# Output projection: the first chunk's mean subtracted by VectorE out of a bank, in place of a product per chunk

## The chip, the cores and the metric

One core of one Trainium2 chip runs the whole program. The metric is the device time of one execution in microseconds. Five engines work side by side, each on its own queue and ordered against the others by semaphores: TensorE (PE: products; PEld: its weight loads), VectorE (DVE), ScalarE (ACT), GpSimd (POOL) and SyncE (SP, which issues the loads of weights). Products land in banks of PSUM, each of 512 fp32 numbers in each of 128 partitions; VectorE and ScalarE read them there.

## The reference, cut to what matters

The kernel is one layer of an encoder for 512 new frames (with 16 meta tokens ahead of them) and 64 frames of a running stream: a layer norm, the input projection, a pooling branch and stick-breaking attention, gates, the output projection, a second layer norm, an MLP and a third layer norm. The change touches the output projection and the layer norm behind it:

```
mix = sigmoid(ga) * (pool_out @ w_br_pool) + sigmoid(gb) * (attn @ w_br_attn)
h   = _layer_norm(ALPHA * h + (mix @ w_out + b_out), ln1_g, ln1_b)

def _layer_norm(x, g, b):
    mu  = mean(x, axis=-1)
    var = mean(square(x - mu), axis=-1)
    return (x - mu) * rsqrt(var + LN_EPS) * g + b
```

A layer norm does not change when the same number is subtracted from all 1024 channels of a token. The kernel uses that: it takes the mean of the first 128 channels off all of them before it sums their squares.

## The kernel before, in words

Activations are kept transposed: channels on the 128 partitions, in 8 chunks (KC = 8), and the 576 tokens (TA) along the free dimension, in two halves of 288 (HA). For accuracy each fp32 operand is split in two parts, hi and lo, and each product of a 128x128 block of weights is three: hi x hi, hi x lo, lo x hi (`kept`, lines 972 to 974). One chunk of output for one half of the tokens is so 8 x 3 = 24 products with 288 columns each.

`out_pass(h)` (line 983) computes the output projection for token half h: out chunks m = 0 to 7, each into bank m % 2 of `lin`. TensorE starts a chunk when the weights are split (`lo_split`, first pass only) and when its bank is free (`bank_free`), which VectorE reports after it has added chunk m - 2 to the residual (`out_half`, line 2137). With two banks VectorE has about one chunk of time for each.

The residual r1 is ready before the projection: ScalarE and VectorE make ALPHA * h + b_out there. `out_half(m, h)` adds the bank to it. After chunk 0, ScalarE writes the negated chunk 0 of the residual into `first_r` (`first_chunk`, line 1491). `ones_r` holds 1/128 everywhere, so the product of ones_r with first_r is the negated mean of the first 128 channels, on every partition. In the kernel before, TensorE adds this product to the bank of every chunk m = 1 to 7 (line 1000) as the last of its accumulation, and once per half into a bank of its own, `r1_shift(h)` (line 1003), out of which VectorE adds it to chunk 0 (`first_shifted`, line 2146). `r1_shift(0)` is bank 2 of `z`, `r1_shift(1)` is `small`.

From the shifted residuals ScalarE makes squares (`square1`), GpSimd sums them and the residuals (`add1`), and TensorE multiplies the two sums by 1/1024 (`r1_sums`). For the first half that product stands behind chunk 0 of the second pass; for the second half it stands behind the first tile of the MLP. VectorE then takes the variance, centres, makes the inverse root and scales chunk by chunk, and ScalarE and VectorE write h_hi and h_lo for the MLP (`norm1_hi`, `norm1_lo`). For the first half all of this lies on VectorE between the evacuations of the second pass, in an order written out by hand (lines 2246 to 2271), along with the splits of the first MLP weights. In the first pass VectorE's queue holds the splits of the projection's weights (`split_out`) and two parts of the residual (`residual_lo`). Before the first `first_chunk`, ScalarE makes the last two parts of its residual and loads a table of functions (lines 1486 to 1495).

Of the kernel before, what the change touches and what calls it, by code (L numbers as in the profile page):

```python
# [8 lines left out]
ALU = mybir.AluOpType  # L9
# [11 lines left out]
KC = D_MODEL // P  # L21
# [135 lines left out]
def encoder_step(nc, x, wstream, w2_d, vecs_d, bv_d, kc_d, vc_d, state_d, wpool_d, y_out, k_out, v_out, s_out):  # L157
    with ExitStack() as ctx:
        base = 16512

        def sb(name, shape, dt, at):

            return nc.alloc_sbuf_tensor_at(name, [P] + shape, dt, offset=base + 4 * at)

        def sem(name):
            return ctx.enter_context(nc.semaphore(name))
# [41 lines left out]
        mix_hi = sb("mix_hi", [KC, TA], F32R, A0 + 13824)  # L208
        mix_lo = sb("mix_lo", [KC, TA], F32R, A0 + 23360)
# [25 lines left out]
        r1 = sb("r1", [KC, TA], F32, A0)  # L235
# [4 lines left out]
        first_r = sb("first_r", [TA], F32R, A0 + 27968 + 7 * TA)  # L240
        ones_r = sb("ones_r", [P], F32R, A0 + 32576)
# [60 lines left out]
        n0_mean, n0_guess, n0_rstd = sem("n0_mean"), sem("n0_guess"), sem("n0_rstd")  # L302
        n0_centred_v, n0_centred_g, n0_scaled, n0_hi, n0_lo = (
            sem("n0_centred_v"), sem("n0_centred_g"), sem("n0_scaled"), sem("n0_hi"), sem("n0_lo"))
        n1_prep1, n1_prep, n1_first, n1_shift, n1_d0 = (
            sem("n1_prep1"), sem("n1_prep"), sem("n1_first"), sem("n1_shift"), sem("n1_d0"))
        n1_sq, n1_sum, n1_sumsq, n1_terms = sem("n1_sq"), sem("n1_sum"), sem("n1_sumsq"), sem("n1_terms")
        n1_msq, n1_mean, n1_var, n1_guess, n1_rstd = (
            sem("n1_msq"), sem("n1_mean"), sem("n1_var"), sem("n1_guess"), sem("n1_rstd"))
# [69 lines left out]
        def vec(col):  # L379
            return vecs[:, bass.ds(col, 1)]  # L380
# [58 lines left out]
        def out_bank(m, p):  # L439

            if m < KEPT2:
                return p, N_MLP2 + m
            i = (KC - KEPT2) * p + m - KEPT2
            return i % 2, N_MLP2 + KEPT2 + i // 2
# [20 lines left out]
        def half(h):  # L465
            return slice(h * HA, (h + 1) * HA)

        def out_home(m):

            if m < 2:  # L470
                return whi[:, m, :], wlo[:, m, :]
            return stay_hi[m // 2 - 1][:, m % 2, :], stay_lo[m // 2 - 1][:, m % 2, :]

        def mlp1_home(j):

            if j < 2:
                return whi[:, j, :], wlo[:, j, :]
            return stay_hi[1][:, j - 2, :], stay_lo[1][:, j - 2, :]
# [7 lines left out]
        def r1_mean(h):  # L486
            return z[:, h, 0:HA]
# [4 lines left out]
        def r1_shift(h):  # L492
            return z[:, 2, 0:HA] if h == 0 else small[:, 0:HA]
# [102 lines left out]
        def _(pe):  # L596
# [372 lines left out]
            def kept(out, home, k, hi, lo, first, last):  # L969

                w_h, w_l = home[0][:, bass.ts(k, P)], home[1][:, bass.ts(k, P)]
                pe.matmul(out, w_h, hi, start=first, stop=False)  # L972
                pe.matmul(out, w_h, lo, start=False, stop=False)  # L973
                return pe.matmul(out, w_l, hi, start=False, stop=last)  # L974

            def r1_sums(h):

                pe.wait_ge(n1_sum, 7 * (h + 1))
                pe.matmul(r1_mean(h), inv_d[:, :], sum1[:, half(h)], start=True, stop=True)
                pe.wait_ge(n1_sumsq, 7 * (h + 1))  # L980
                pe.matmul(r1_sq(h), inv_d[:, :], sumsq1[:, half(h)], start=True, stop=True).then_inc(n1_terms, 1)

            def out_pass(h):

                c = half(h)
                for m in range(KC):
                    bank = lin[:, m % 2, 0:HA]
                    if h == 0:
                        pe.wait_ge(lo_split, U_OUT + m + 1)
                    pe.wait_ge(bank_free[m % 2], N_OUT + 4 * h + m // 2)  # L990
                    for k in range(KC):
                        if m == 0:
                            pe.wait_ge(mix_lo_done, 2 * k + h + 1)
                        last = kept(bank, out_home(m), k, mix_hi[:, k, c], mix_lo[:, k, c], k == 0,
                                    m == 0 and k == KC - 1)
                    if m:
                        if m == 1:
                            pe.wait_ge(ones_made, 1)
                            pe.wait_ge(n1_first, h + 1)
                        last = pe.matmul(bank, ones_r[:, :], first_r[:, c], start=False, stop=True)  # L1000
                    last.then_inc(unit_done if h else half_done, 1)
                    if m == 1:
                        pe.matmul(r1_shift(h), ones_r[:, :], first_r[:, c], start=True, stop=True)\
                            .then_inc(n1_shift, 1)
                    if h == 1 and m == 0:
                        r1_sums(0)

# [3 lines left out]
            def mlp1_kept(j, h, k):  # L1011

                c = slice(META + h * HA, META + (h + 1) * HA)
                return kept(lin[:, j % 2, 0:HA], mlp1_home(j), k, h_hi[:, k, c], h_lo[:, k, c], k == 0, k == KC - 1)

            for j in range(4):
                pe.wait_ge(lo_split, U_MLP1[0] + j + 1)
                pe.wait_ge(bank_free[j % 2], N_MLP1[0] + j // 2)
                for k in range(KC):
                    if j == 0:  # L1020
                        pe.wait_ge(n1_lo, k + 1)
                    last = mlp1_kept(j, 0, k)
# [3 lines left out]
            for k in range(KC + LAG):  # L1026
                if k < KC:
# [3 lines left out]
                    last = mlp1_kept(0, 1, k)  # L1031
                    if k == KC - 1:
                        last.then_inc(unit_done, 1)
                if k >= LAG:
                    if k == LAG:
                        pe.wait_ge(bank_free[1], N_MLP1[0] + 2)
                    last = mlp1_kept(1, 1, k - LAG)
            last.then_inc(unit_done, 1)
            for j in range(2, 4):
                pe.wait_ge(bank_free[j % 2], N_MLP1[0] + 3)  # L1040
                for k in range(KC):
                    last = mlp1_kept(j, 1, k)
# [82 lines left out]
            for m in range(KEPT2):  # L1125
                for h in range(2):
                    bank, before = out_bank(m, h)
# [8 lines left out]
            for p, c in enumerate(PARTS2):  # L1136
                for m in range(KEPT2, KC):
                    bank, before = out_bank(m, p)
# [626 lines left out]
        def _(dve):  # L1765
            tt = nc.vector.tensor_tensor
# [17 lines left out]
            def split_kept(u, home):  # L1784

                dve.wait_ge(hi_split, u + 1)
                tt(home[1], raw[:, u % RAW, :], home[0].bitcast(F32), ALU.subtract).then_inc(lo_split, 1)
# [174 lines left out]
            for m in range(4):  # L1962
# [4 lines left out]
                for e in range(2):  # L1967
                    rows = slice(64 * e, 64 * e + 64)
                    last = nc.vector.tensor_scalar(q_s[rows, 2 * m + e, :], lin[rows, 1, SEQ - HA:HA],
                                                   vecs[rows, V_BIN + C_Q + m:V_BIN + C_Q + m + 1], SB_SCALE,  # L1970
                                                   ALU.add, ALU.mult)
# [135 lines left out]
            def split_out(m):  # L2107
                split_kept(U_OUT + m, out_home(m))

            def residual_lo(m):  # L2110

                dve.wait_ge(n1_prep1, m + 1)
                stt(out=r1[:, m, :], in0=h_lo[:, m, META:T].bitcast(F32), scalar=ALPHA, in1=r1[:, m, :],
                    op0=ALU.mult, op1=ALU.add).then_inc(n1_prep, 1)
# [22 lines left out]
            def out_half(m, h):  # L2137

                if h == 0:
                    dve.wait_ge(half_done, N_OUT + m + 1)  # L2140
                    dve.wait_ge(n1_prep, m + 1)
                else:
                    dve.wait_ge(unit_done, U_OUT + m + 1)
                tt(r1[:, m, half(h)], lin[:, m % 2, 0:HA], r1[:, m, half(h)], ALU.add).then_inc(bank_free[m % 2], 1)

            def first_shifted(h):

                dve.wait_ge(n1_shift, h + 1)
                tt(r1[:, 0, half(h)], r1_shift(h), r1[:, 0, half(h)], ALU.add).then_inc(n1_d0, 1)
# [10 lines left out]
            def centre1(h):  # L2160


                dve.wait_ge(n1_mean, h + 1)
                for k in range(BY_DVE1):
                    tt(r1[:, k, half(h)], r1[:, k, half(h)], r1_mean(h), ALU.subtract).then_inc(n1_centred_v, 1)
# [21 lines left out]
            def norm1_lo(k, h):  # L2187

                cc = slice(META + h * HA, META + (h + 1) * HA)
                dve.wait_ge(n1_hi, KC * h + k + 1)  # L2190
                stt(out=h_lo[:, k, cc], in0=r1[:, k, half(h)], scalar=vec(V_LN1_B + k),
                    in1=h_hi[:, k, cc].bitcast(F32), op0=ALU.add, op1=ALU.subtract).then_inc(n1_lo, 1)
# [41 lines left out]
            def split_mlp1(j):  # L2234
                split_kept(U_MLP1[0] + j, mlp1_home(j))

            split_out(2)
            for m in range(KC):
                out_half(m, 0)
                if m in (1, 2):  # L2240
                    residual_lo(5 + m)
                if m == 1:
                    first_shifted(0)
                if m + 3 < KC:
                    split_out(m + 3)
            out_half(0, 1)
            split_mlp1(0)
            variance1(0)
            centre1(0)
            out_half(1, 1)  # L2250
            first_shifted(1)
            inverse1(0)
# [1 line left out]
            scale1(1, 0)  # L2254
            norm1_lo(0, 0)
            split_mlp1(1)
            out_half(2, 1)
            for k in (2, 3, 4):
                scale1(k, 0)
                norm1_lo(k - 1, 0)  # L2260
            out_half(3, 1)
            for k in (5, 6, 7):
                scale1(k, 0)
                norm1_lo(k - 1, 0)
            out_half(4, 1)
            norm1_lo(7, 0)
            split_mlp1(2)
            out_half(5, 1)
            split_mlp1(3)
            out_half(6, 1)  # L2270
            out_half(7, 1)

            first_tile(0, 0)
# [449 lines left out]
```

## Time and profile before

| | us |
|---|---|
| median of 3 runs | 816.35 (815.94 to 817.53) |
| profiled execution | 816.22 |
| its span | 814.2 |
| TensorE busy | 799.0 (98%) |
| VectorE busy | 495.2 (61%) |
| ScalarE busy | 388.9 (48%) |
| GpSimd busy | 100.3 (12%) |
| mean granted TensorE clock | 0.995 of full speed |
| first pass of the projection, first product | 354.63 |
| second pass, first product | 381.04 |
| first product of the MLP | 408.60 |

The span is the time from the first to the last instruction of the profile; the execution's own time is about 2 us longer. The last three lines are points of time from the span's start, read in the timeline. Products are pipelined: the profile gives each a duration of 0.29 us, though the next one starts well before it ends. An engine's busy time counts overlapped instructions once. In a timeline a bracket at the end of a row says how long the engine was idle ahead of it and for whom it waited.

### The profile page before, as it was taken

The page shows a single profiled execution, that of the slowest core. Times are in us where ns is not written, and L with a number is a line of the kernel's source. Part 1 is how long each engine was busy: PE and PEld are TensorE (multiplying, and loading weights), DVE is VectorE, ACT ScalarE, POOL GpSimd, SP SyncE. Part 2 cuts the span into 40 slices and gives each one's busy share as a digit, 9 for nine tenths or more (in the row PEclk, how much of TensorE's full clock was granted, in tenths as well). Part 3 has the DMA queues.
Part 4 walks back from the last instruction along what each step waited for, and adds up shares of the span by engine and source line. Part 5 has one row for each costly group of instructions (what it writes and reads, how often), then busy time and mean ns, then how long its engine had stood idle before and what let it go on. Part 6 is the DMA issues. An engine that isn't in the chain of part 4 may idle for free.

```text
span 814.2 us, 14502 instructions
## 1 busy us (share of the span) xinstructions
PE 799.0 (98%) x5892; PEld 767.9 (94%) x5893; DVE 495.2 (61%) x829; ACT 388.9 (48%) x646; POOL 100.3 (12%) x120
## 2 busy tenths in 40 slices
PE   8999999999999999999999999999999999999994
PEld 6999899988988899999999999999999999999994
DVE  5823454553535376874977678775667877445444
ACT  4623345554646475563555663334455333344334
POOL 2100000660000000006720000000000000000444
PEclk9999999999999999999999999999999999999997
DMA  8632131112111112243202214222321422223102
GB/s 297 264 135 84 52 112 52 59 50 78 53 52 53 52 52 78 79 131 104 85 20 78 65 39 155 79 104 78 100 69 39 155 78 105 78 79 95 60 14 103
DMA packets 23081, 71.61 MB, mean 88 GB/s; under 512 B 2464, under 2 KB 6704, under 8 KB 22640
## 3 DMA queue, kind: packets, MB, share of 16 engines
q1 hardware_dynamic: 22336, 68.23, 25.2%
q0 software_dynamic: 544, 2.52, 0.9%
q8 instruction: 40, 0.66, 0.3%
q14 instruction: 17, 0.14, 0.1%
q10 hardware_dynamic: 144, 0.07, 0.0%
HBM read 65.96 MB, written 4.85 MB: 87 GB/s over the span
## 4 chain that ended last, share of the span: by engine, by line
PE 96%; DVE 2%; ACT 1%; DMA 1%; issue 0%; SPq 0%; ACTq 0%; DVEq 0%
PE lin L603 14%; PE lin L604 14%; PE lin L605 14%; PE z L1067 6%; PE z L1069 5%; PE z L1070 5%; PE z L840 3%; PE lin L972 3%; PE lin L973 3%; PE lin L974 3%; PE lin L1088 2%; PE lin L1086 2%; PE lin L1087 2%; PE z L826 1%; PE z L901 1%; PE lin L723 1%
## 5 line engine op out<-in xcount | busy, mean ns | idle before, releaser
L603 PE MATMUL lin<-h_hi,whi 128*128 128x288 f32 (+1 forms) x832 | 247.3, 297 | 0.0
L604 PE MATMUL lin<-h_lo,whi 128*128 128x288 f32 (+1 forms) x832 | 245.9, 296 | 0.0
L605 PE MATMUL lin<-h_hi,wlo 128*128 128x288 f32 (+1 forms) x832 | 245.0, 294 | 0.0
L605 PEld LDWEIGHTS lin<-h_hi,wlo 128*128 128x128 f32 x832 | 156.6, 188 | 0.0
L603 PEld LDWEIGHTS lin<-h_hi,whi 128*128 128x128 f32 x832 | 156.4, 188 | 0.1
L604 PEld LDWEIGHTS lin<-h_lo,whi 128*128 128x128 f32 x832 | 156.4, 188 | 0.1
L1772 DVE TENSOR_TENSOR wlo<-raw,whi 128x1024 fp32r<-128x1024 f32 x65 | 80.9, 1245 | 34.9 <-ACT whi L1162 30.0
L1162 ACT ACTIVATE whi<-raw 128x1024 fp32r<-128x1024 f32 x58 | 60.9, 1051 | 50.5 <-PE lin L605 32.5
L1565 ACT ACTIVATE relu_t<-lin,vecs 128x288 f32<-128x288 f32 x60 | 30.0, 500 | 91.4 <-PE lin L605 88.0
L2196 DVE TENSOR_TENSOR relu_sq<-relu_t 128x288 f32<-128x288 f32 x60 | 27.4, 457 | 64.8 <-ACT relu_t L1565 64.8
L1067 PE MATMUL z<-f_ops,whi 128*128 128x288 f32 x216 | 64.0, 296 | 1.0 <-issue 1.0
L1069 PE MATMUL z<-f_ops,whi 128*128 128x288 f32 x216 | 63.5, 294 | 0.0
L1070 PE MATMUL z<-f_ops,wlo 128*128 128x288 f32 x216 | 63.0, 291 | 0.0
L1612 ACT ACTIVATE whi<-w_set 128x768 fp32r<-128x768 f32 x36 | 30.4, 846 | 52.8 <-PE z L1070 42.5
L2643 POOL TENSOR_TENSOR sum<-r 128x576 f32<-128x576 f32 x1 | 1.4, 1438 | 346.4 <-DVE r L2417 346.4
L1067 PEld LDWEIGHTS z<-f_ops,whi 128*128 128x128 f32 x216 | 40.5, 188 | 1.4 <-issue 1.4
L1070 PEld LDWEIGHTS z<-f_ops,wlo 128*128 128x128 f32 x216 | 40.7, 188 | 0.0
L2335 DVE TENSOR_TENSOR wlo<-w_set,whi 128x768 fp32r<-128x768 f32 x36 | 34.5, 957 | 10.0 <-ACT whi L1612 10.0
L1069 PEld LDWEIGHTS z<-f_ops,whi 128*128 128x128 f32 x216 | 40.5, 188 | 0.0
L1991 DVE SCALAR_TENSOR_TENSOR sa<-z,sa 128x512 f32<-128x512 f32 (+4 forms) x25 | 19.8, 793 | 26.9 <-ACT sa L1338 26.9
L1069 PE MATMUL z<-f_ops,third_hi 128*128 128x288 f32 x120 | 35.6, 297 | 0.0
L1070 PE MATMUL z<-f_ops,third_lo 128*128 128x288 f32 x120 | 35.2, 293 | 0.0
(338 smaller groups left out, 1887.5 us busy)
## 6 DMA issues: line engine op xcount, KB each, us to landing
raw<-w_stream SPq DMA_DIRECT2D x88, 512.0 KB, 3.5
w_set<-w_sets SPq DMA_DIRECT2D x32, 384.0 KB, 3.7
r<-x_t SPq DMA_DIRECT2D x8, 296.0 KB, 5.0
kcache<-k_cache SPq DMA_DIRECT2D x1, 2048.0 KB, 10.2
vcache<-v_cache SPq DMA_DIRECT2D x1, 2048.0 KB, 10.3
y<-r SPq DMA_DIRECT2D x8, 160.0 KB, 1.8
k_new<-k_t POOLq DMA_DIRECT2D x1, 1184.0 KB, 4.8
v_new<-v_t POOLq DMA_DIRECT2D x1, 1024.0 KB, 5.2
```

The lines of the kernel that those rows point to most:

```text
L603: pe.matmul(out, w_h, hi, start=first, stop=False)
L604: pe.matmul(out, w_h, lo, start=False, stop=False)
L605: return pe.matmul(out, w_l, hi, start=False, stop=last)
L1067: pe.matmul(out, w_h, f_op(f, i, 0), start=opens and i == 0, stop=False, skip_group_check=True)
L1069: pe.matmul(out, w_h, f_op(f, i, 1), start=False, stop=False, skip_group_check=True)
L1070: last = pe.matmul(out, w_l, f_op(f, i, 0), start=False, stop=i == PRS - 1, skip_group_check=True)
L1162: nc.scalar.activation(whi[:, j % SPLIT, :], raw[:, j, :], ACT.Copy).then_inc(hi_split, 1)
L1565: nc.scalar.activation(dst, lin[:, bank, 0:HA], ACT.Relu, bias=vec(V_B1 + u)).then_inc(bank_free[bank], 1)
L1612: nc.scalar.activation(op_home(o)[0], w_set[g % 2][:, i, :], ACT.Copy).then_inc(s_hi, 1)
L1772: tt(wlo[:, j % SPLIT, :], raw[:, j, :], whi[:, j % SPLIT, :].bitcast(F32), ALU.subtract)\
L2196: tt(dst, src, src, ALU.mult).then_inc(f_sq_done, 1)
L2335: tt(home[1], w_set[g % 2][:, RAW_SLOT[q], :], home[0].bitcast(F32), ALU.subtract).then_inc(s_lo, 1)
```

## The change

The product per chunk is gone. The one product of ones_r and first_r that is left goes into the bank r1_shift(h), and stands in the middle of chunk 1 (after k = 3) in place of behind it; the wait for first_r moves with it. VectorE adds that bank to the residual of each of the chunks 1 to 7 in an instruction of its own, `shifted1(m, h)`, which waits for the shift product and for the residual to be prepared, and reports to a new semaphore `n1_shifted`. `out_half(m, h)` waits for it. In VectorE's hand-written order the first half's additions of chunks 1 and 2 stand ahead of out_half(1, 0), those of chunks 3 to 7 behind out_half(1, 0) to out_half(5, 0); in the second half shifted1(1, 1) and shifted1(2, 1) stand directly ahead of their out_half, and shifted1(m, 1) for m = 3 to 7 behind out_half(m - 1, 1).

```diff
                     for k in range(KC):
                         if m == 0:
                             pe.wait_ge(mix_lo_done, 2 * k + h + 1)
-                        last = kept(bank, out_home(m), k, mix_hi[:, k, c], mix_lo[:, k, c], k == 0,
-                                    m == 0 and k == KC - 1)
-                    if m:
-                        if m == 1:
+                        if m == 1 and k == KC // 2:
                             pe.wait_ge(ones_made, 1)
                             pe.wait_ge(n1_first, h + 1)
-                        last = pe.matmul(bank, ones_r[:, :], first_r[:, c], start=False, stop=True)
+                            pe.matmul(r1_shift(h), ones_r[:, :], first_r[:, c], start=True, stop=True)\
+                                .then_inc(n1_shift, 1)
+                        last = kept(bank, out_home(m), k, mix_hi[:, k, c], mix_lo[:, k, c], k == 0, k == KC - 1)
                     last.then_inc(unit_done if h else half_done, 1)
-                    if m == 1:
-                        pe.matmul(r1_shift(h), ones_r[:, :], first_r[:, c], start=True, stop=True)\
-                            .then_inc(n1_shift, 1)
...
+                if m:
+                    dve.wait_ge(n1_shifted, 7 * h + m)
                 tt(r1[:, m, half(h)], lin[:, m % 2, 0:HA], r1[:, m, half(h)], ALU.add).then_inc(bank_free[m % 2], 1)
+
+            def shifted1(m, h):
+
+                dve.wait_ge(n1_shift, h + 1)
+                dve.wait_ge(n1_prep, m + 1)
+                tt(r1[:, m, half(h)], r1_shift(h), r1[:, m, half(h)], ALU.add).then_inc(n1_shifted, 1)
...
             for m in range(KC):
+                if m == 1:
+                    shifted1(1, 0)
+                    first_shifted(0)
+                    shifted1(2, 0)
                 out_half(m, 0)
                 if m in (1, 2):
                     residual_lo(5 + m)
-                if m == 1:
-                    first_shifted(0)
+                if m and m + 2 < KC:
+                    shifted1(m + 2, 0)
                 if m + 3 < KC:
                     split_out(m + 3)
...
             centre1(0)
+            shifted1(1, 1)
             out_half(1, 1)
...
             split_mlp1(1)
+            shifted1(2, 1)
             out_half(2, 1)
+            shifted1(3, 1)
...
             out_half(3, 1)
+            shifted1(4, 1)
...
             out_half(4, 1)
+            shifted1(5, 1)
...
             out_half(5, 1)
+            shifted1(6, 1)
             split_mlp1(3)
             out_half(6, 1)
+            shifted1(7, 1)
             out_half(7, 1)
```

## Rows read from the trace of the kernel before

**Rows 1.** Page, part 1: busy us (share of span) xinstructions, by engine
```profile
PE 799.0 (98%) x5892; PEld 767.9 (94%) x5893; DVE 495.2 (61%) x829; ACT 388.9 (48%) x646; POOL 100.3 (12%) x120
```

**Rows 2.** Waits of PE over the whole span: us in total, times, longest
```profile
PE lin L720 <- ACT h_hi L1257: 1.4, 1, 1.4
```

**Rows 3.** Windows: length, busy us (xcount) by engine, PEclk (granted), DMA
```profile
15.00:20.00 5.00, 2.99 (x14) 1.93 (x13) 4.24 (x10) 2.53 (x6) 2.86 (x9) 1.00 0.79 268
381.04:408.60 27.56, 27.56 (x206) 27.35 (x205) 20.49 (x37) 13.47 (x26) 17.30 (x18) 1.00 0.24 76
805.00:810.00 5.00, 0.00 (x0) 0.00 (x0) 4.90 (x14) 3.06 (x8) 2.56 (x4) 0.56 0.07 26
```

**Rows 4.** Line 1000: duration ns min/median/max, first and last start
```profile
L1000 PE MATMUL lin<-first_r,ones_r x14: 292/294/297, 361.0 to 408.5; 128*128 128x288 f32 x14
```

**Rows 5.** Timeline of PE, first pass, chunk 1: start us, us
```profile
357.83 0.29 PE L972 MATMUL lin<-mix_hi,whi 128*128 128x288 f32 x1
359.43 0.29 PE L972 MATMUL lin<-mix_hi,whi 128*128 128x288 f32 x1
361.02 0.29 PE L1000 MATMUL lin<-first_r,ones_r 128*128 128x288 f32 x1
361.28 0.30 PE L972 MATMUL lin<-mix_hi,stay_hi 128*128 128x288 f32 x1
```

**Rows 6.** Timeline of PE, second pass, and first product of the MLP
```profile
384.21 0.65 PE L979 MATMUL z<-sum,inv_d 128*128 128x288 f32 x2
386.75 0.30 PE L972 MATMUL lin<-mix_hi,whi 128*128 128x288 f32 x1
...
395.27 0.29 PE L972 MATMUL lin<-mix_hi,stay_hi 128*128 128x288 f32 x1
401.94 0.29 PE L972 MATMUL lin<-mix_hi,stay_hi 128*128 128x288 f32 x1
408.60 0.29 PE L972 MATMUL lin<-h_hi,whi 128*128 128x288 f32 x1
```

**Rows 7.** Timeline of ACT: before and at the negated copies of chunk 0
```profile
358.92 1.28 ACT L1182 ACT_TABLE_LOAD   x1
360.21 0.45 ACT L1494 ACTIVATE first_r<-r 128x288 fp32r<-128x288 f32 x1
...
385.43 0.43 ACT L1494 ACTIVATE first_r<-r 128x288 fp32r<-128x288 f32 x1
```

**Rows 8.** Timeline of DVE, second pass
```profile
389.36 0.44 DVE L2149 TENSOR_TENSOR r<-small,r 128x288 f32<-128x288 f32 x1
389.73 0.44 DVE L2171 SCALAR_TENSOR_TENSOR sumsq<-var,sumsq 128x288 f32<-128x288 f32 x1
390.21 0.95 DVE L2174 SCALAR_TENSOR_TENSOR z<-sumsq,rstd 128x288 f32<-128x288 f32 x1
...
393.89 0.45 DVE L2144 TENSOR_TENSOR r<-lin,r 128x288 f32<-128x288 f32 x1
...
397.74 1.03 DVE L2191 SCALAR_TENSOR_TENSOR h_lo<-r,vecs,h_hi 128x288 fp32r<-128x288 f32 x1
...
400.53 0.44 DVE L2144 TENSOR_TENSOR r<-lin,r 128x288 f32<-128x288 f32 x1
...
403.27 0.44 DVE L2144 TENSOR_TENSOR r<-lin,r 128x288 f32<-128x288 f32 x1
```

**Rows 9.** Timeline of POOL: last sum of squares of the first half
```profile
382.54 0.80 POOL L2621 TENSOR_TENSOR sumsq<-sumsq,sq 128x288 f32<-128x288 f32 x1
```

**Rows 10.** Timeline of PE and DVE: restarts of PE after waits
```profile
17.77 0.37 PE L720 MATMUL lin<-h_hi,whi 128*128 128x296 f32 x1 [1.44 <-ACT h_hi L1257]
...
18.91 0.52 DVE L1916 SCALAR_TENSOR_TENSOR h_lo<-r,vecs,h_hi 128x296 fp32r<-128x296 f32 x1
...
19.49 0.41 PE L723 MATMUL lin<-h_lo,whi 128*128 128x296 f32 x1 [0.57 <-DVE h_lo L1916]
19.74 0.29 PE L720 MATMUL lin<-h_hi,whi 128*128 128x296 f32 x1
```

More of the change, by code:

```diff
@@ L304, in encoder_step @@
             sem("n0_centred_v"), sem("n0_centred_g"), sem("n0_scaled"), sem("n0_hi"), sem("n0_lo"))
-        n1_prep1, n1_prep, n1_first, n1_shift, n1_d0 = (
-            sem("n1_prep1"), sem("n1_prep"), sem("n1_first"), sem("n1_shift"), sem("n1_d0"))
+        n1_prep1, n1_prep, n1_first, n1_shift, n1_d0, n1_shifted = (
+            sem("n1_prep1"), sem("n1_prep"), sem("n1_first"), sem("n1_shift"), sem("n1_d0"), sem("n1_shifted"))
         n1_sq, n1_sum, n1_sumsq, n1_terms = sem("n1_sq"), sem("n1_sum"), sem("n1_sumsq"), sem("n1_terms")
```

## The prediction

> **What bounds the kernel now.** I read the page's busy shares first: TensorE is busy 98% of the span [rows 1], so a product saved is worth its time only while nothing makes TensorE wait. The waits of TensorE come next: seven in the whole kernel, the longest of 1.4 us [rows 2], at 17.77 [rows 10], and none at a line of the output projection. The stretch of the projection's second pass says the same, TensorE busy all 27.56 us, but it also shows VectorE busy 20.49 us of them [rows 3], far over its 61% of the span: the engine that gets the new work has little room here. The timelines then give the distances.
>
> **The products removed.** Fourteen products of line 1000 go [rows 4]. Their 294 ns is latency, not cost: consecutive starts matter. From 359.43 to 361.02 TensorE starts twelve products, 0.133 us apart [rows 5]; from 395.27 to 401.94 it starts 50, again 0.133 apart, line 1000's two among them [rows 6]. The removal is worth 14 x 0.133 = 1.86 us if TensorE never waits. Seven are in each pass. The two products of line 1003 stay; they only move.
>
> **The shift product moved (first pass).** It used to stand behind all 24 products of chunk 1, and now stands behind twelve. It reads first_r, which ScalarE writes. The queue there does not change: table load at 358.92 for 1.28 us, then the copy from 360.21 to 360.66 [rows 7]. Nothing that feeds it moves, since TensorE, VectorE and ScalarE do the same work as before up to that point. TensorE arrives at 359.43 instead of 361.02 [rows 5]. It arrived 0.36 us after the copy before; now it arrives 1.23 us ahead of it. A restart after a wait costs something too: VectorE's instruction ends at 18.91 + 0.52 = 19.43, the waiting product starts at 19.49 and the next at 19.74, 0.25 later instead of 0.133 [rows 10], so 0.18 us in all behind the release. The stall is 1.23 + 0.18 = 1.41 us. What queues behind it is the second half of chunk 1, and with it everything of TensorE. Bounds: 1.23 with a free restart, 1.5 with a dearer one. With the first pass's seven products gone (-0.93) the second pass starts 1.41 - 0.93 = 0.48 us later than before.
>
> **VectorE in the first pass.** Seven adds of 128x288 out of the shift's bank. The nearest row is first_shifted, the same operands: 0.44 us, and the next instruction starts 0.37 later [rows 8]. They go between splits for which VectorE waited before, and TensorE comes 1.3 us later to chunk 2, so I cost them at nothing; if that cover went, each is 0.37.
>
> **The shift product moved (second pass).** TensorE reaches it at 386.75 + 0.48 = 387.23 [rows 6]; the copy ends at 385.43 + 0.43 + 0.48 = 386.34 [rows 7]. No wait. Nor for the statistics: the last sum of squares ended at 383.34 [rows 9], 0.87 ahead of the product that reads it at 384.21 [rows 6]; both move by about 0.5.
>
> **VectorE in the second pass.** This is the large term. VectorE does the first half's normalisation here and is behind TensorE. A bank must be evacuated by out_half(m) before TensorE starts chunk m + 2. The slack before, start of the chunk less the end of the evacuation: chunk 4 395.27 - 394.34 = 0.93; chunk 6 401.94 - 400.97 = 0.97; chunk 7 (one chunk of 25 products, 3.33, after 401.94) 405.27 - 403.71 = 1.56 [rows 6, 8]. The change takes from it on both sides. VectorE has two more adds before out_half(2), four before out_half(4), five before out_half(5), 0.37 each. And shifted1(1) and shifted1(2) stand directly ahead of the evacuation that waits for their result: a dependent pair starts 0.48 apart, an independent one 0.37 (389.36, 389.73, 390.21) [rows 8], so 2 x 0.11 = 0.22 more. TensorE in turn comes earlier by 0.133 for every removed product: three by chunk 4, five by chunk 6, six by chunk 7. With 0.18 for the restart:
> chunk 4: 0.93 - 0.74 - 0.22 - 0.40 - 0.18 = -0.61
> chunk 6: 0.97 - 1.48 - 0.22 - 0.67 - 0.18 = -1.58
> chunk 7: 1.56 - 1.85 - 0.22 - 0.80 - 0.18 = -1.49
> Stalls accumulate, so the pass loses the largest shortfall, 1.58 us, in pieces ahead of chunks 4 to 6, and chunk 7 then finds its bank just free. Shifted1(6) and shifted1(7) fall where VectorE waited, and are hidden. Behind the pass nothing is added for VectorE and the second half's normalisation keeps its distance to TensorE. Bounds: 0 if VectorE makes up what it is late (it can't drop work: 20.49 busy of 27.56 [rows 3], but some of it is stretched); upward 1.6 more if instructions with both inputs in SBUF are stretched more often by GpSimd (next part). I take 1.58, which is the sum of rows.
>
> For the pairs, the rows show 0.48 against 0.37 [rows 8]. The Trainium skill, "VectorE: DVE Perf Modes", section "The DRAIN you can't avoid", says that between VectorE instructions "the semaphore costs nothing extra". By that rule the pairs would cost no 0.22 and the pass would lose 1.36; the trace disagrees with it for a pair in which the second waits for the first, and the sum goes by the trace.
>
> **Sum.** -1.86 + 1.41 + 1.58 = +1.13 us. The profiled execution took 816.22 us (span 814.2 and 2.0 around it), 0.13 under the median of the runs, 816.35. I predict 816.22 + 1.13 = 817.35, 817.4. 0.2% (1.6 us) is about what a measurement of this kernel can tell from no change, so this counts as no change.
>
> **The rivals.**
> A, only the first pass stalls. For it: the second pass's excess rests on many short VectorE instructions, and one was stretched from about 0.5 to 1.03 while GpSimd worked [rows 8]; were the stretched ones fewer, the slack is wider. Against: they all have to be missed at once. -1.86 + 1.41 = -0.45: 815.8.
> B, faster: neither stall, since ScalarE's copy comes early enough. -1.86: 814.4. For it: TensorE waited nowhere here before [rows 2]. Against: the table load ahead of the copy ends at 360.20 [rows 7] and nothing shortens it. With a smaller first stall and none in the second pass it would still be hardly faster.
> C, slower: VectorE's backlog grows by contention with GpSimd. GpSimd's sums wait for ScalarE's squares, which wait behind VectorE's normalisation; pushed later they overlap more of VectorE's two-SBUF-input instructions. The second instruction of the inverse took 0.95 and one h_lo 1.03 where about 0.5 is usual [rows 8]; three more of these before out_half(4) add 1.5 us. It decides against me from 0.5 us on: +1.13 + 1.5 = +2.6: 818.9. The Trainium skill, "SBUF — State Buffer", section "Who interferes with whom", calls the port that VectorE and GpSimd share an exclusive lock, which a VectorE instruction with two SBUF inputs contends for; the two long rows agree, and by it the new adds, with one input in PSUM, are not stretched themselves.
> D, the stalls cost TensorE its clock. It fell to 0.56 of full speed in a stretch in which TensorE did nothing; in a stretch with 2.99 us busy of 5, and the 1.4 us wait in it, it stayed at 1.00 [rows 3, 10]. The new stalls are no longer than that. If it fell to the lower of the two levels (1.2 of 2.4 GHz) for some 25 products, that is 3.3 us more: 820.7.
> E, the change doesn't do what it says: the shift product with its adds is there but a product per chunk stays. The diff removes them; no weight.
>
> **How the numbers follow.** The forecast (both stalls) 0.62, A 0.14, B 0.05, C 0.16, D 0.03. The forecast's own range is 816.4 to 818.4 (second stall 0.7 to 2.5). The range that holds 8 in 10 takes in A at 815.8 and the lower part of C: 815.4 to 818.8. Faster by over 0.2% needs B nearly whole, and what the measurement adds: 0.09. Slower by over 0.2%, above 818.0: C and D, 0.19, and a fifth of the forecast's 0.62, so 0.31. The rest, 0.60, is no change.
>
> **What would show it.** No product of first_r into lin. In the first pass TensorE waits once, 1.2 to 1.5 us, for ScalarE's first_r ahead of the shift product. In the second pass TensorE waits for VectorE's r ahead of chunks 4, 5 and 6, 1 to 2 us together, and the largest share before chunk 6; no such wait before chunk 7 over 0.3. The MLP's first product starts at 409.7 instead of 408.60 [rows 6], and everything after it keeps that distance. I am wrong if TensorE waits only once (A), if it doesn't wait (B), if the waits of the second pass sum to over 2.5 us with longer wlo and h_lo rows (C), or if the granted clock dips around 361 or 400 (D).

## The result, and the profile after

The changed kernel took 819.03 us in the median of 22 runs (817.27 to 821.25), the kernel before 816.94 in as many beside it. One of the latter took 2776.16 us; the other 21 have a median of 816.62 (815.94 to 818.48), and the ratio goes by them: 1.0022, 95% interval 1.0014 to 1.0029, which is +1.1 to +2.4 us. The prediction was 817.4 in a range from 815.4 to 818.8, made from three runs of the kernel before with a median of 816.35; on that footing the ratio gives 818.1, inside the range. The bare median of 819.03 is above it. The direction is that of the forecast, the size larger than its +1.1, just over the 0.2% that the forecast took for no change, with an interval on both sides of it. The profiled execution's span is 2.9 longer (817.1, before 814.2). Where these differ is shown below: the projection itself lost 1.24 us, the rest is from elsewhere in the kernel.

The page's first part after (it answers to [rows 1]). TensorE's busy time is hardly changed although products are gone: the profile models the end of each product, so that short waits behind it count as busy, and some stretches elsewhere ran slower (below). It can't be used to tell what was won. VectorE has fourteen more instructions.

```profile
PE 799.4 (98%) x5879; PEld 767.2 (94%) x5879; DVE 501.5 (61%) x843; ACT 389.0 (48%) x646; POOL 99.9 (12%) x120
```

TensorE's waits after, answering to [rows 2]. The columns are us in total, times, longest. Two of them are new: one for ScalarE's copy, and one for VectorE's evacuations; shorter waits of the second kind hide in the modelled ends of the products and are read from the starts below.

```profile
PE lin L720 <- ACT h_hi L1253: 1.4, 1, 1.4
PE z L997 <- ACT first_r L1490: 1.2, 1, 1.2
...
PE lin L972 <- DVE r L2142: 0.5, 1, 0.5
```

The timelines of TensorE in the first pass and of ScalarE, answering to [rows 5] and [rows 7]. The shift product is now line 997, the copy line 1490.

```profile
359.43 0.29 PE L972 MATMUL lin<-mix_hi,whi 128*128 128x288 f32 x1
360.89 0.29 PE L974 MATMUL lin<-mix_hi,wlo 128*128 128x288 f32 x1
362.40 0.37 PE L997 MATMUL z<-first_r,ones_r 128*128 128x288 f32 x1 [1.22 <-ACT first_r L1490]
362.61 0.30 PE L972 MATMUL lin<-mix_hi,whi 128*128 128x288 f32 x1
...
364.21 0.29 PE L972 MATMUL lin<-mix_hi,stay_hi 128*128 128x288 f32 x1
```

```profile
360.52 1.28 ACT L1178 ACT_TABLE_LOAD   x1
361.81 0.44 ACT L1490 ACTIVATE first_r<-r 128x288 fp32r<-128x288 f32 x1
```

TensorE reaches the shift product at about 361.02 (its twelfth product of the chunk starts at 360.89), and starts it at 362.40, 0.15 behind the end of the copy at 361.81 + 0.44. The next product follows 0.21 later. The table load of 1.28 us stands right ahead of the copy.

The second pass of TensorE, answering to [rows 6]. The rows are the first products of chunk 0 and of chunks 4, 5, 6 and 7, and the last is the MLP's first product:

```profile
383.17 0.29 PE L972 MATMUL lin<-mix_hi,whi 128*128 128x288 f32 x1
...
397.64 0.40 PE L972 MATMUL lin<-mix_hi,stay_hi 128*128 128x288 f32 x1 [0.49 <-DVE r L2142]
...
401.06 0.40 PE L972 MATMUL lin<-mix_hi,stay_hi 128*128 128x288 f32 x1
...
404.63 0.40 PE L972 MATMUL lin<-mix_hi,stay_hi 128*128 128x288 f32 x1
...
408.13 0.40 PE L972 MATMUL lin<-mix_hi,stay_hi 128*128 128x288 f32 x1
...
411.44 0.29 PE L972 MATMUL lin<-h_hi,whi 128*128 128x288 f32 x1
```

24 products at 0.133 are 3.20 us. From 401.06 to 404.63 are 3.57, and from 404.63 to 408.13 3.50: the chunks wait for their banks, each product starting within 0.1 us of the end of the evacuation that frees its bank. VectorE in the same stretch, answering to [rows 8]:

```profile
396.57 0.45 DVE L2148 TENSOR_TENSOR r<-small,r 128x288 f32<-128x288 f32 x1
397.12 0.46 DVE L2142 TENSOR_TENSOR r<-lin,r 128x288 f32<-128x288 f32 x1
397.50 0.45 DVE L2148 TENSOR_TENSOR r<-small,r 128x288 f32<-128x288 f32 x1
...
401.72 0.66 DVE L2195 SCALAR_TENSOR_TENSOR h_lo<-r,vecs,h_hi 128x288 fp32r<-128x288 f32 x1
...
404.14 0.44 DVE L2142 TENSOR_TENSOR r<-lin,r 128x288 f32<-128x288 f32 x1
...
404.87 1.09 DVE L2195 SCALAR_TENSOR_TENSOR h_lo<-r,vecs,h_hi 128x288 fp32r<-128x288 f32 x1
405.88 1.83 DVE L1783 TENSOR_TENSOR stay_lo<-raw,stay_hi 128x1024 fp32r<-128x1024 f32 x1
407.64 0.45 DVE L2142 TENSOR_TENSOR r<-lin,r 128x288 f32<-128x288 f32 x1
```

Line 2142 is the evacuation; that of chunk 2 ends at 397.12 + 0.46 = 397.58, and chunk 4 starts at 397.64. That of chunk 4 ends at 404.58 (chunk 6 starts at 404.63), that of chunk 5 at 408.09 (chunk 7 at 408.13). VectorE's share of the pass has grown from the 20.49 of 27.56 us in [rows 3] to:

```profile
383.17:411.44 28.27, 27.64 (x200) 26.52 (x199) 23.52 (x44) 13.35 (x26) 15.47 (x18) 1.00 0.20 59
```

One measure serves for all that follows, the **distance** from the first product of chunk 1 in the first pass to the MLP's first product. It is 408.60 - 357.83 = 50.77 us before [rows 5, 6] and 411.44 - 359.43 = 52.01 after: +1.24. In parts: the first pass (to the first product of the second) went from 23.21 to 23.74, the second from 27.56 to 28.27. Behind the distance both kernels take the same (814.2 - 408.60 = 405.6 and 817.1 - 411.44 = 405.7 to the span's end); over the thirteen profiles of this study that remainder is 405.6 to 406.8, and the changed kernel has both 405.7 and, profiled again, 406.8. The traces show where these 1.2 us arise: in two stretches of the MLP, 94 to 144 and 238 to 288 us behind its first product, some executions start 379 or 380 products in 50 us and others 383 or 384, at a granted clock of 1.00 and with TensorE busy throughout. Each slow stretch costs 0.6 us; six profiles have none, five one, two both. The first of these stretches in the kernel before, and in the changed kernel profiled again:

```profile
502.60:552.60 50.00, 50.00 (x383) 50.00 (x383) 37.93 (x53) 18.22 (x21) 0.00 (x0) 1.00 0.23 77
```

```profile
503.98:553.98 50.00, 50.00 (x380) 50.00 (x379) 37.38 (x53) 18.23 (x21) 0.00 (x0) 1.00 0.23 76
```

What makes the products start farther apart there is not shown.

**What is not the change's.** The other 1.6 us of the profiled execution lie ahead of the projection (359.43 against 357.83), in work that both kernels have in common. They arise before 30 us; from there to the projection the two profiles stay 1.6 apart. The stretch from 15 to 25 us, first before, then changed (the columns are those of [rows 3]):

```profile
15.00:25.00 10.00, 7.99 (x44) 6.45 (x43) 9.02 (x21) 6.93 (x14) 2.86 (x9) 1.00 0.88 316
```

```profile
15.00:25.00 10.00, 7.99 (x35) 6.38 (x33) 8.97 (x22) 6.97 (x15) 3.19 (x9) 0.83 0.86 312
```

The granted clock was 1.00 before and 0.83 in the changed kernel, the lower of the two levels (1.2 of 2.4 GHz) for a third of the stretch. TensorE had been busy 2.0 of the 4 us from 16 to 20 us, and the clock of 20 to 22 us was 0.50. The changed kernel profiled again had 1.00 there. Of the thirteen profiles five have 0.83, and they start chunk 1 of the first pass at 358.8 to 359.4; the eight with 1.00 start it at 357.3 to 358.6. Both kinds hold several kernels, and the changed kernel is in both, so this is a matter of the execution. It splits the runs of either kernel: of those with a mean granted clock of 0.995 or more, 8 of the changed kernel have a median of 817.74 and 18 of the kernel before (measured with the first experiments) 816.39, 1.35 apart, near the 1.24 of the profiles; the others, 14 and 17, have 819.65 and 818.02. The changed kernel had 14 of its 22 runs in the second group, which adds to the ratio, but only 4 of 12 when it was run again; so nothing ties the group to the change. (For the runs of the kernel before that the ratio rests on, the clock is not on record.)

### The profile page after: what moved, and what is told of

Same layout as the page of the kernel before. It is cut to its first block, busy times and chain, and to the rows that moved or that the text cites. A ratio compares the mean times of both kernels' runs of the same rounds, so it can differ in the third digit from the quotient of the medians.

```text
span 817.1 us, 14510 instructions
## 1 busy us (share of the span) xinstructions
PE 799.4 (98%) x5879; PEld 767.2 (94%) x5879; DVE 501.5 (61%) x843; ACT 389.0 (48%) x646; POOL 99.9 (12%) x120
## 4 chain that ended last, share of the span: by engine, by line
PE 93%; DVE 4%; ACT 2%; issue 1%; DMA 1%; SPq 0%; ACTq 0%; DVEq 0%
PE lin L603 14%; PE lin L604 14%; PE lin L605 14%; PE z L1063 6%; PE z L1065 5%; PE z L1066 5%; PE z L840 3%; PE lin L972 2%; PE lin L973 2%; PE lin L974 2%; PE lin L1084 2%; PE lin L1082 2%; PE lin L1083 2%; PE z L826 1%; PE z L901 1%; PE lin L723 1%
```

## The experiments

All distances are of one profiled execution each, which repeats well: the changed kernel profiled again gave 52.01, first pass 23.74, second 28.27, as above. Times are medians, with the ratio to the runs of the kernel before that ran beside them.

| kernel | distance | 1st pass | 2nd pass | median us | ratio (95% interval) |
|---|---|---|---|---|---|
| before | 50.77 | 23.21 | 27.56 | | |
| changed | 52.01 | 23.74 | 28.27 | 819.03 | 1.0022 (1.0014 to 1.0029) |
| changed, again | 52.01 | 23.74 | 28.27 | 818.67 | 1.0019 (1.0008 to 1.0029) |
| shift product late | 50.81 | 22.52 | 28.29 | 817.91 | 1.0007 (0.9993 to 1.0021) |
| first pass only | 50.08 | 22.52 | 27.56 | 816.81 | 0.9992 (0.9982 to 1.0002) |
| second pass only | 51.49 | 23.22 | 28.27 | 818.20 | 1.0015 (1.0004 to 1.0026) |
| move only | 52.22 | 24.66 | 27.56 | 818.40 | 1.0017 (1.0008 to 1.0026) |
| copy ahead of load | 51.24 | 22.97 | 28.27 | 818.31 | 1.0009 (0.9998 to 1.0020) |
| pairs apart | 51.64 | 23.74 | 27.90 | 818.11 | 1.0015 (1.0003 to 1.0027) |
| two more additions | 52.67 | 23.75 | 28.92 | 819.54 (1 run) | |
| order only | 50.77 | 23.21 | 27.56 | 817.38 | 1.0008 (0.9998 to 1.0017) |
| reordered | 49.33 | 22.52 | 26.81 | 815.14 | 0.9977 (0.9967 to 0.9986) |
| reordered, both passes | 49.56 | 22.74 | 26.82 | 815.65 | 0.9985 (0.9976 to 0.9995) |

The distance resolves 0.1 us; the times do not. Their intervals are 1.2 to 2.3 us wide, since the start and the remainder vary from one execution to the next, and the ratios stand from 0.4 us under to 0.7 over what the distance says.

**The changed kernel again.**

> The changed kernel once more, beside the variants. Theory: distance from the first product of chunk 1 in the first pass to the MLP's first product 52.0 us as before, 1.24 over the kernel before; executions in which the granted TensorE clock is 0.995 or more 1.2 to 1.4 us over those of the kernel before with the same clock. Rival 1 (much of the change's time is lost at the kernel's start): distance under 51.5 with a time 2 us over.

The distance came out as before. The runs at a clock of 0.995 or more are 1.6 over those of the kernel before (818.55 against 816.95), a little more than was expected; the profiled one of them has both slow stretches of the MLP.

**Shift product late.** In the first pass it stands behind chunk 1 again:

```diff
-                        if m == 1 and k == KC // 2:
+                        if h == 1 and m == 1 and k == KC // 2:
...
                     last.then_inc(unit_done if h else half_done, 1)
+                    if m == 1 and h == 0:
+                        pe.wait_ge(ones_made, 1)
+                        pe.wait_ge(n1_first, h + 1)
+                        pe.matmul(r1_shift(h), ones_r[:, :], first_r[:, c], start=True, stop=True)\
+                            .then_inc(n1_shift, 1)
```

> The change with the first pass's shift product back behind all 24 products of chunk 1. Distance from the first product of chunk 1 in the first pass to the MLP's first product: 50.77 us in the kernel before, 52.01 in the changed one. Theory (two stalls): the wait for ScalarE's copy goes, the waits for VectorE in the second pass stay at 1.4 to 1.7 us; distance 50.77 - 1.86 + 1.6 = 50.5, time 0.3 us under the kernel before. Rival 1 (the time is lost at the kernel's start, not here): the distance falls too but the time stays some 2 us over the kernel before. Rival 2 (VectorE's adds in the first pass cost something too): distance over 51.

The wait for the copy is gone and the second pass is as it was (28.29), so the two losses are independent. (The time, 0.6 over the kernel before with an interval of 2.3, can't tell the 0.3 less that was expected.) The first pass is 22.52, not the 23.21 - 0.93 = 22.28 that seven saved products give. TensorE and VectorE at the start of chunk 3:

```profile
365.28 0.29 PE L974 MATMUL lin<-mix_hi,stay_lo 128*128 128x288 f32 x1
365.57 0.37 PE L972 MATMUL lin<-mix_hi,stay_hi 128*128 128x288 f32 x1
365.77 0.30 PE L973 MATMUL lin<-mix_lo,stay_hi 128*128 128x288 f32 x1
```

```profile
363.88 0.45 DVE L2153 TENSOR_TENSOR r<-z,r 128x288 f32<-128x288 f32 x1
364.25 0.45 DVE L2158 TENSOR_TENSOR r<-z,r 128x288 f32<-128x288 f32 x1
364.61 0.45 DVE L2153 TENSOR_TENSOR r<-z,r 128x288 f32<-128x288 f32 x1
364.98 0.45 DVE L2147 TENSOR_TENSOR r<-lin,r 128x288 f32<-128x288 f32 x1
```

The evacuation of chunk 1 stands behind three additions and ends at 365.43, and chunk 3 starts at 365.57 where 365.41 was due; 0.24 in all with the restart and chunk 4. The prediction had costed the first pass's additions at nothing. In the changed kernel they were in fact hidden, but only because TensorE was held up by the copy.

**First pass only, and second pass only.** In each, one pass is that of the changed kernel (the first with the late shift product) and the other that of the kernel before:

```diff
                         last = kept(bank, out_home(m), k, mix_hi[:, k, c], mix_lo[:, k, c], k == 0,
-                                    m == 0 and k == KC - 1)
-                    if m:
+                                    k == KC - 1 and (h != 1 or m == 0))
+                    if m and h == 1:
...
+                if m and h == 0:
+                    dve.wait_ge(n1_shifted, m)
```

The diff is against the kernel before and is that for the first pass only; for the second pass only the three conditions have h != 0, h == 0 and h == 1. Of the shifted1 calls only those of the changed pass are there.

> Only the first pass's seven products are replaced by VectorE's adds, with the shift product behind chunk 1; the second pass is that of the kernel before. Theory: TensorE waits nowhere in the projection, distance 50.77 - 0.93 = 49.84, time 0.9 us under the kernel before. Rival 1: time not under the kernel before although the distance is. Rival 2: VectorE's adds in the first pass hold up the second one, distance over 50.3.

> Only the second pass is changed; the first is that of the kernel before. Theory: waits for VectorE of 1.6 us ahead of chunks 4, 5 and 6 against 0.93 saved, distance 50.77 + 0.65 = 51.4, time 0.6 to 0.7 us over the kernel before. Rival 1: time 2 us over it or equal to it, without that distance. Rival 2 (the backlog comes from the first pass): no waits here, distance 49.84.

The second pass alone is 28.27, to the hundredth that of the changed kernel, behind a first pass of 23.22 without a wait. Its loss is its own and not a backlog carried over. The first alone keeps 0.69 of its 0.93. Both times agree with it: 0.7 us under the kernel before, which by its interval (1.5 under to 0.2 over) could also be nothing, and 1.2 over it with an interval of 0.3 to 2.1.

**Move only.** The kernel before with all its products, and the shift product of the first pass in the middle of chunk 1.

```diff
+                        if h == 0 and m == 1 and k == KC // 2:
+                            pe.wait_ge(ones_made, 1)
+                            pe.wait_ge(n1_first, h + 1)
+                            pe.matmul(r1_shift(h), ones_r[:, :], first_r[:, c], start=True, stop=True)\
+                                .then_inc(n1_shift, 1)
...
-                        if m == 1:
-                            pe.wait_ge(ones_made, 1)
+                        if m == 1 and h == 1:
                             pe.wait_ge(n1_first, h + 1)
...
-                    if m == 1:
+                    if m == 1 and h == 1:
                         pe.matmul(r1_shift(h), ones_r[:, :], first_r[:, c], start=True, stop=True)\
                             .then_inc(n1_shift, 1)
```

> The kernel before with one thing moved: the first pass's shift product stands in the middle of chunk 1; every chunk keeps its product. Theory: one wait of 1.2 us for ScalarE's copy, 1.4 to 1.5 with the restart; distance 50.77 + 1.45 = 52.2, time 1.4 us over the kernel before. Rival 1: time 0 or over 2.5 us more. Rival 2 (the wait is made up later, for example by chunks that no longer wait): distance under 51.5.

```profile
360.90 0.37 PE L997 MATMUL z<-first_r,ones_r 128*128 128x288 f32 x1 [1.22 <-ACT first_r L1498]
```

The same wait of 1.22, and 24.66 - 23.21 = 1.45 us lost. Nothing later gives it back.

**Copy ahead of the table load.** The changed kernel with one line of ScalarE moved:

```diff
-            use_tables(EXP_AND_LN)
...
             first_chunk(0)
+            use_tables(EXP_AND_LN)
```

> The changed kernel with one thing moved on ScalarE: the negated copy of chunk 0 of the first half stands ahead of the table load. Theory (the load is what makes TensorE wait): the copy ends some 0.9 to 1.0 us earlier, TensorE's wait at the shift product falls from 1.22 to about 0.3, distance 52.0 - 1.0 = 51.0. Rival (VectorE's addition of chunk 0 is late too, or the copy needs the table): wait of 1.2 as now, distance 52.0.

```profile
359.56 0.37 PE L997 MATMUL z<-first_r,ones_r 128*128 128x288 f32 x1 [0.24 <-ACT first_r L1488]
```

The wait fell from 1.22 to 0.24 and the first pass by 0.77, not 1.0: with TensorE earlier, chunks 3 and 4 start 0.12 and 0.08 late, much as in the late version. The load is what made the copy late.

**Pairs apart.**

```diff
             shifted1(1, 1)
-            out_half(1, 1)
             first_shifted(1)
+            out_half(1, 1)
...
-            split_mlp1(1)
             shifted1(2, 1)
+            split_mlp1(1)
             out_half(2, 1)
```

> The changed kernel with the two dependent pairs of the second pass pulled apart: first_shifted(1) between shifted1(1) and out_half(1), the split of the second MLP weights between shifted1(2) and out_half(2). The same work. The pairs now start 0.55 apart, where independent ones start 0.37 apart. Theory (the dependence costs 0.18 each): VectorE is 0.36 earlier from there on, distance 52.0 - 0.36 = 51.65. Rival (waiting for the own result costs nothing): 52.0, the starts merely move.

```profile
389.41 0.44 DVE L2148 TENSOR_TENSOR r<-small,r 128x288 f32<-128x288 f32 x1
389.78 0.44 DVE L2153 TENSOR_TENSOR r<-small,r 128x288 f32<-128x288 f32 x1
390.14 0.44 DVE L2142 TENSOR_TENSOR r<-lin,r 128x288 f32<-128x288 f32 x1
390.51 0.44 DVE L2175 SCALAR_TENSOR_TENSOR sumsq<-var,sumsq 128x288 f32<-128x288 f32 x1
```

Three additions and the instruction behind them now start 0.37 apart where the pair in the changed kernel was 0.55 apart (396.57 to 397.12), and the pass is 0.37 shorter, as much as two pairs of 0.18: the whole of it reaches the end. The Trainium skill, "VectorE: DVE Perf Modes", section "The DRAIN you can't avoid", has the semaphore cost "nothing extra"; for an instruction that waits for the one just ahead of it, these runs show 0.18 us.

**Two more additions.**

```diff
             shifted1(4, 1)
+            for scratch in (mean1, rstd1):
+                tt(scratch[:, half(1)], r1_shift(1), r1[:, 1, half(1)], ALU.add).then_inc(spare, 1)
```

> The changed kernel with two more additions of the same shape on VectorE behind shifted1(4) in the second pass; their results go to places that nothing reads before they are written again. Theory (VectorE's queue sets the second pass's end): two of 0.37 us, distance 52.0 + 0.7 = 52.7. Rival (TensorE's waits come from something else, such as the hand-over between engines): distance unchanged at 52.0.

```profile
405.16 0.40 PE L972 MATMUL lin<-mix_hi,stay_hi 128*128 128x288 f32 x1 [0.76 <-DVE r L2142]
```

The two additions are 0.73 us of VectorE's time and the distance grew by 0.66, with the wait ahead of chunk 6, which follows the next evacuation. VectorE's queue sets this pass's end.

**Order only.** The kernel before with the splits of the MLP's weights 1, 2 and 3 later:

```diff
-            split_mlp1(1)
             out_half(2, 1)
...
             norm1_lo(7, 0)
+            split_mlp1(1)
-            split_mlp1(2)
             out_half(5, 1)
+            split_mlp1(2)
-            split_mlp1(3)
             out_half(6, 1)
             out_half(7, 1)
+            split_mlp1(3)
```

> The kernel before with the same later places of the MLP's weight splits on VectorE as in the reordered version, and nothing else. Theory (the order has no gain of its own, since TensorE waits nowhere here): distance 50.77, time that of the kernel before. Rival (the reordered version's gain is the order's): time 1 us or more under the kernel before.

The distance is the kernel before's to the hundredth, and the time is not under it.

**Reordered.** The changed kernel with the late shift product, and VectorE's second pass as follows:

```diff
             shifted1(1, 1)
+            first_shifted(1)
             out_half(1, 1)
-            first_shifted(1)
...
-            split_mlp1(1)
             shifted1(2, 1)
+            shifted1(3, 1)
             out_half(2, 1)
-            shifted1(3, 1)
...
+            shifted1(4, 1)
             out_half(3, 1)
-            shifted1(4, 1)
...
+            shifted1(5, 1)
             out_half(4, 1)
-            shifted1(5, 1)
             norm1_lo(7, 0)
-            split_mlp1(2)
+            split_mlp1(1)
+            shifted1(6, 1)
             out_half(5, 1)
-            shifted1(6, 1)
-            split_mlp1(3)
+            split_mlp1(2)
+            shifted1(7, 1)
             out_half(6, 1)
-            shifted1(7, 1)
             out_half(7, 1)
+            split_mlp1(3)
```

> A version meant to keep the gain: the changed kernel with the first pass's shift product behind all 24 products of chunk 1, and with VectorE's second pass in another order: each shifted1 ahead of work that doesn't depend on it, and the splits of the MLP's weights 1, 2 and 3 behind out_half(4), out_half(5) and out_half(7). Theory: no waits in the second pass, and in the first the 0.25 seen with this place of the product: distance 50.77 - 1.86 + 0.25 = 49.2, time 1.6 us under the kernel before. Rival 1: VectorE is simply too full, waits of 1 us or more stay. Rival 2: the late splits make the MLP wait at its products 2 to 4, so that the gain is given back behind the distance measured.

```profile
397.21 0.30 PE L972 MATMUL lin<-mix_hi,stay_hi 128*128 128x288 f32 x1
...
400.51 0.40 PE L972 MATMUL lin<-mix_hi,stay_hi 128*128 128x288 f32 x1
...
403.80 0.29 PE L972 MATMUL lin<-mix_hi,stay_hi 128*128 128x288 f32 x1
```

Chunks 5, 6 and 7 start 3.30 and 3.29 us apart, 0.1 over their 3.20 each: that is what is left of the second pass's waits. The distance is 1.44 under the kernel before, of 1.86 to be had, and the time 0.9977 of it (0.9967 to 0.9986), 1.9 us less. It beats both kernels. The second rival falls too: over the first 60 us of the MLP TensorE starts its products at the same distances from the first as in the kernel before, to 0.1 us, so the late splits hold nothing up.

**Reordered, both passes.** The same, and in the first pass:

```diff
                     first_shifted(0)
-                    shifted1(2, 0)
                 out_half(m, 0)
+                if m == 1:
+                    shifted1(2, 0)
```

> The reordered version, and in the first pass out_half(1) stands ahead of shifted1(2) on VectorE, which frees the bank of chunk 3 one addition (0.37) earlier. Theory: the 0.25 us of waits left in the first pass go, distance 49.33 - 0.25 = 49.1, time 1.8 us under the kernel before. Rival (those 0.25 are no wait for VectorE): distance 49.33.

It didn't help: chunk 3 now starts on time, but chunk 4 waits, and the first pass is 22.74 instead of 22.52. VectorE's and GpSimd's rows of this version, then those of the reordered one:

```profile
365.41 1.29 DVE L2114 SCALAR_TENSOR_TENSOR r<-h_lo,r 128x576 f32<-128x576 f32 x1
...
365.27 0.81 POOL L2637 TENSOR_TENSOR sum<-r 128x288 f32<-128x288 f32 x1 [188.28 <-DVE r L2147]
```

```profile
364.09 0.75 DVE L2114 SCALAR_TENSOR_TENSOR r<-h_lo,r 128x576 f32<-128x576 f32 x1
...
364.25 1.25 POOL L2636 TENSOR_TENSOR sum<-r 128x288 f32<-128x288 f32 x1 [188.58 <-DVE r L2147]
```

The evacuation of chunk 1 also releases GpSimd's first sum. Made earlier, that sum starts 0.14 ahead of residual_lo (the row of 128x576), which then takes 1.29, and the evacuation that frees chunk 4's bank stands behind it; in the reordered version residual_lo starts first and takes 0.75, and the sum is the one stretched, to 1.25 from 0.81. Whoever starts first goes on, and the other stands. The Trainium skill, "SBUF — State Buffer", section "Who interferes with whom", has it as an exclusive lock; both orders agree with it.

## Why the prediction was right, and where it was off

- **The products removed, 1.86 us.** Right: chunks of the first pass take 3.16 where they took 3.30 [rows 5], those of the second 3.20 where they took 3.33 [rows 6].
- **The first stall, 1.41.** Measured 23.74 - 23.21 + 0.93 = 1.46, in the predicted place and with the predicted wait of 1.22 for the copy. The move alone costs the same, and with the copy ahead of the load nearly all of the wait goes. This step is shown. (TensorE's waits before were eight on seven lines, and not seven [rows 2]; nothing hangs on it.)
- **VectorE in the first pass, 0.** Right for the changed kernel, where TensorE's wait covered it. The clause on that cover was too loose: without it the cost is not 0.37 each but 0.24 in all.
- **The second stall, 1.58.** Measured 28.27 - 27.56 + 0.93 = 1.64. The mechanism is right, but that the size is so near is in part luck, since three errors nearly cancel. Over 3.20, chunks 4 to 7 started 0.65, 0.22, 0.37 and 0.30 late, the MLP 0.11; the largest piece was foretold ahead of chunk 6 and came ahead of chunk 4. By chunk 6 that is 1.24, less than the 1.58 foretold: out_half(4) stood 1.48 us later in its pass than before (404.14 - 383.17 against 400.53 - 381.04) and not 1.70, since the dependent pairs cost 0.18 each and not 0.11, but the h_lo that took 1.03 before [rows 8] now took 0.66; and only 0.05 of the 0.18 for the restart falls ahead of the chunk. By chunk 7 it is 1.54 where 1.49 was foretold, but as a binding wait: out_half(5) stood 2.24 us later (407.64 - 383.17 against 403.27 - 381.04) where 2.07 was foretold, because the h_lo ahead of it took 1.09 and the split 1.83. Before the change they had taken:

```profile
400.90 0.70 DVE L2191 SCALAR_TENSOR_TENSOR h_lo<-r,vecs,h_hi 128x288 fp32r<-128x288 f32 x1
401.73 1.62 DVE L1787 TENSOR_TENSOR stay_lo<-raw,stay_hi 128x1024 fp32r<-128x1024 f32 x1
```

  Contention with GpSimd moved from one instruction to others; that it is contention is read from the overlap, as in this row of GpSimd, which starts 0.04 ahead of the h_lo that took 1.09:

```profile
404.83 0.80 POOL L2631 TENSOR_TENSOR sum<-sum,r 128x288 f32<-128x288 f32 x1
```

  Rival C had the mechanism, but the sum of it hardly changed, and no slower case came from it in the projection.
- **The sum, +1.13.** The distance grew by 1.24. (The MLP's first product, foretold at 409.7, stands at 411.44, 1.6 of it from ahead of the projection.) The ratio's +1.8 (1.1 to 2.4) has that near its lower end. What the sum left out is that the rest of the kernel is not fixed: by the profiles it moves by a microsecond at the start, with the clock, and by up to 1.2 behind the distance. That the ratio came out above the projection's 1.24 is most likely this; no run shows how it splits. The range's upper end was drawn from the projection's terms alone.
- **Rivals.** A and B fall: both stalls are there. So does E: the products of first_r into lin are gone from the projection. D's mechanism, the clock, did appear, but not at these waits: the granted clock stayed at 1.00 in the projection (last column but two of the row of the second pass above), and at 361 us in all thirteen profiles. The reading behind D's small chance was weak, though: that a stretch with 2.99 us busy of 5 leaves the clock at 1.00 [rows 3] was true of that execution, while in the changed kernel's profile the same stretch, again with 2.99 busy, is the one behind which the clock fell.

## What to carry to other kernels

A product saved on the engine that bounds a kernel is worth the distance between two starts, not its listed duration, and only as long as the engine that takes over the work keeps its deadlines; so write down each buffer's slack (next user's start less the release) before moving work, and subtract from both sides. Moving an instruction forward in a queue moves it past nothing only if its operand is ready: look at what stands ahead of the operand's producer. Where the receiving engine is late, first move out of its way what has a later deadline; here the new order of VectorE was worth 1.48 us (distance 50.81 to 49.33), and with the late shift product it turned a loss of 1.24 us into a gain of 1.44.

## What was not expected of the hardware

- An addition out of PSUM (128x288) that waits for the result of the one just ahead of it on VectorE starts 0.55 us after it, an independent one 0.37 us.
- Freeing a buffer 0.37 us earlier made the projection 0.23 us slower (49.33 to 49.56), because GpSimd's sum then started 0.14 us ahead of a VectorE instruction with both inputs in SBUF, which took 1.29 in place of 0.75 us.
- The same kernel has executions with a granted TensorE clock of 0.83 and of 1.00 in the stretch from 15 to 25 us. The first reach the projection about a microsecond later.
- Two stretches of 50 us in the MLP, with TensorE busy throughout at a granted clock of 1.00, hold 383 or 384 products in some executions and 379 or 380 in others, whatever the kernel.
